# Two-layer conv, pooling and expert-retrieval encoder on one core: part of a norm's summing moved to VectorE, reciprocal roots spread without diagonal matrices, pooled products and four convolution taps moved to ScalarE

## The reference

```python
for l in range(DEPTH):                                   # DEPTH = 2
    mod = cond @ w_ada[l] + b_ada[l]                     # six vectors: shift, scale, gate, twice
    h = modulate(rmsnorm(x, norm1_g[l]), sh1, sc1)
    z = h @ w_in[l]                                      # 1024 -> 1536
    ya = conv_mixer(z[..., :512], z[..., 512:1024], ...) # u = a * sigmoid(b); 31 causal taps; LayerNorm; silu
    yb = pool_mixer(z[..., 1024:], ...)                  # y = (pooled @ w_grp + b_grp) * scale, 4 groups of 128
    x = x + g1 * (concat(ya, yb) @ w_out[l])             # 1024 -> 1024
    h = modulate(rmsnorm(x, norm2_g[l]), sh2, sc2)
    x = x + g2 * peer(h, peer_wq[l], ...)                # top-16 retrieval from 16384 experts
return rmsnorm(x, final_g)
```

## Time and profile before

| what | value |
|---|---|
| median of 3 runs | 3412.71 us (3411.85 to 3416.69) |
| the profiled execution, its own time | 3411.68 us |
| its span, first to last instruction | 3409.5 us |
| PE busy | 3326.1 us, 98% of the span |
| DVE, ACT, POOL busy | 2399.7, 1142.2, 746.4 us |
| mean granted clock of PE | 0.99 |
| PE idle, all waits of the list together | 75 us |

### The profile page before, as it was taken

One profiled execution on the slowest core, in us unless ns is written; L12 is line 12 of the kernel. 1 busy time (PEld: TensorE's weight loads), 2 busy tenths in 40 slices (PEclk: granted clock), 3 DMA queues, 4 the chain that ended last, 5 costly groups with the idle time before them and its releaser, 6 DMA issues.

```text
span 3409.5 us, 55288 instructions
## 1 busy us (share of the span) xinstructions
PE 3326.1 (98%) x16402; PEld 2815.3 (83%) x16402; DVE 2399.7 (70%) x6143; ACT 1142.2 (33%) x1606; POOL 746.4 (22%) x445
## 2 busy tenths in 40 slices
PE   6989999999999999999999999999999999999998
PEld 4568888888888999999975788888888889999997
DVE  7972999699994456666686259924999844666665
ACT  3233222334443333333342332223444433333332
POOL 0033454400000013333101334442000000233330
PEclk8999999999999999999999999999999999999999
DMA  6163766445556668888721224444555476788884
GB/s 245 51 220 108 251 229 218 153 180 203 184 222 225 203 230 283 282 286 279 231 97 38 75 90 148 146 147 140 186 204 222 176 245 202 255 286 281 282 285 142
DMA packets 316570, 675.88 MB, mean 198 GB/s; under 512 B 28864, under 2 KB 176704, under 8 KB 314304
## 3 DMA queue, kind: packets, MB, share of 16 engines
q1 hardware_dynamic: 253248, 478.81, 42.6%
q10 hardware_dynamic: 40704, 128.88, 9.6%
q0 software_dynamic: 22528, 67.19, 5.2%
HBM read 546.66 MB, written 127.93 MB: 198 GB/s over the span
## 4 chain that ended last, share of the span: by engine, by line
PE 83%; DVE 11%; issue 4%; DMA 1%; ACT 1%; DVEq 0%; SPq 0%; ACTq 0%
PE bank L481 27%; PE bank L605 24%; PE bank L485 13%; PE bank L609 12%; PE bank L588 3%; DVE scratch L1201 1%; DVE scratch L1086 1%; PE bank L405 1%; DVE h L1179 1%; DVE h L1182 1%; DMA scratch<-ada_t 1%; DVE h L1178 1%; DVE h L1181 1%; DVE z_pad L1228 1%; DVE z_pad L1230 1%
## 5 line engine op out<-in xcount | busy, mean ns | idle before, releaser
L481 PE MATMUL bank<-h_hi,w_hi 128*128 128x512 f32 x2528 | 1000.2, 396 | 5.1 <-ACT scratch L644 2.3
L481 PE MATMUL bank<-h_lo,w_hi 128*128 128x512 f32 x2528 | 985.5, 390 | 0.0
L644 ACT ACTIVATE w_hi<-ring 128x1024 fp32r<-128x1024 f32 x584 | 614.5, 1052 | 1106.1 <-PE bank L485 1060.1
L605 PE MATMUL bank<-v_hi,w_hi 128*128 128x448 f32 x2032 | 742.1, 365 | 0.0
L605 PE MATMUL bank<-v_lo,w_hi 128*128 128x448 f32 x2032 | 742.1, 365 | 0.0
L865 POOL TENSOR_TENSOR w_lo<-ring,w_hi 128x1024 fp32r<-128x1024 f32 x172 | 446.4, 2596 | 855.7 <-ACT w_hi L644 855.5
L485 PE MATMUL bank<-h_hi,w_lo 128*128 128x512 f32 x2528 | 624.3, 389 | 0.0
L481 PEld LDWEIGHTS bank<-h_hi,w_hi 128*128 128x128 f32 x2528 | 474.8, 188 | 105.9 <-issue 4.9
L481 PEld LDWEIGHTS bank<-h_lo,w_hi 128*128 128x128 f32 x2528 | 474.8, 188 | 98.3 <-issue 2.4
L485 PEld LDWEIGHTS bank<-h_hi,w_lo 128*128 128x128 f32 x2528 | 474.5, 188 | 98.5
L886 POOL DMA_INDIRECT keys<-ga_scratch,keys x128 | 122.3, 956 | 1623.1 <-DVE v_lo L1323 1623.1
(11 more groups left out here) (169 smaller groups left out, 2458.8 us busy)
## 6 DMA issues: line engine op xcount, KB each, us to landing
ring<-u_t SPq DMA_DIRECT2D x256, 512.0 KB, 3.5
ring<-v_t SPq DMA_DIRECT2D x256, 512.0 KB, 5.8
ga_scratch<-norm_tmp ACTq DMA_DIRECT2D x256, 256.0 KB, 2.0
g_scratch<-scratch ACTq DMA_DIRECT2D x14, 4096.0 KB, 13.7
scratch<-ga_scratch SPq DMA_DIRECT2D x256, 224.0 KB, 4.1
scratch<-g_scratch SPq DMA_DIRECT2D x128, 448.0 KB, 4.2
scratch<-ada_t SPq DMA_DIRECT2D x76, 512.0 KB, 5.7
ring<-wq_t SPq DMA_DIRECT2D x32, 512.0 KB, 3.3
```

What stands on the lines that cost most here:

```text
L481: pe.matmul(to, w_hi[:, b, k * P:(k + 1) * P], part_h[:, k, :], start=(k == 0 and part_h is h_hi), stop=False)
L605: pe.matmul(bank[:, k, 0:TD], w_hi[:, b, k * P:(k + 1) * P], part_w[:, b, 0:TD], start=(first and part_w is v_hi), stop=False)
L644: return act.activation(to, of, ACT.Copy)
```

## The change

Norm 2: PE no longer sums every square. DVE adds the squares of tiles 1 to 5 (`ADDED`) into that of tile 0 while `wout` runs, one before each of the tiles 3 to 7, and PE sums three at the end (blocks 0, 6 and 7). All norms: L974 goes; PE spreads the roots with four matmuls whose stationary operand is one column repeated 128 times and whose moving operand is the identity. Norm 2's order on DVE: the roots come first, then layer 0's last modulation, the biases and the gains. The bias adding becomes another form of instruction. Mixers: ACT makes taps 0 and 1 of conv blocks 1 and 2 (`begin_taps`, after `win` tiles 6 and 11), and takes the pooled products twice out of PSUM, to `mix` and to `h_hi`, with a bias made beforehand.

```diff
+    ADDED = 5
-    GATED_AT = {18: 1, 32: 2, 48: 3}
+    GATED_AT = {18: 1, 34: 2, 50: 3}
+    BEGUN = 2
@@ PE, spread_roots
-                pe.wait_ge(diag_ready, n_root + 1)
-                pe.matmul(bank[:, 1, :], ones[:, :], norm_tmp[:, 0, :], start=True, stop=True).then_inc(spread, 1)
+                pe.wait_ge(roots_made, n_root + 1)
+                for a in range(TT):
+                    root_a = norm_tmp[:, 1, 2 * TT + a:2 * TT + a + 1]
+                    mm = pe.matmul(bank[:, 1, a * P:(a + 1) * P], root_a.to_broadcast([P, P]), ident[:, :],
+                                   start=True, stop=True)
+                mm.then_inc(spread, 1)
@@ PE, wout
-                    if n == 2:
-                        sum_square(2 * l + 1, 0)
-                    sum_square(2 * l + 1, n - 1)
-                sum_square(2 * l + 1, KC - 1)
+                pe.wait_ge(square_added, ADDED * l + ADDED)
+                for n, k in enumerate([0] + list(range(ADDED + 1, KC))):
+                    pe.wait_ge(squared, KC * (2 * l + 1) + (k + 1))
+                    mm = sums(sq, n, k, KC - ADDED - 1)
+                mm.then_inc(summed, 1)
@@ ACT, win and mixers
+                BEGIN_AT = {6: 1, N_WIN - 1: 2}
+                def begin_taps(j):
+                    act.wait_ge(u_ready, CONV * l + (j + 1))
+                    at = COL_CONVW + j * TAPS
+                    act.activation(conv_y[:, j, :], u_pad[:, j, 0:T], ACT.Identity, scale=small[:, at:at + 1],
+                                   bias=small[:, COL_CONVB + j:COL_CONVB + j + 1])
+                    if j >= 2:
+                        act.wait_ge(conv_ready, (CONV - 1) * l + (j - 1))
+                    act.activation(conv_y[:, CONV - 1, :] if j == 1 else conv_odd, u_pad[:, j, 1:1 + T], ACT.Copy,
+                                   scale=small[:, at + 1:at + 2]).then_inc(taps_begun, 1)
...
+                    if n in BEGIN_AT:
+                        begin_taps(BEGIN_AT[n])
...
+                act.wait_ge(pool_bias_ready, l + 1)
                 for g in range(CONV):
-                    act.wait_ge(mix_b_ready, CONV * l + (g + 1))
-                    copy(h_hi[:, CONV + g, :], mix[:, CONV + g, :]).then_inc(hi_ready_h, 1)
+                    act.wait_ge(pool_product, CONV * l + (g + 1))
+                    for to in (mix, h_hi):
+                        ins = act.activation(to[:, CONV + g, :], bank[:, 4 + g, :], ACT.Identity, bias=pool_bias[:, g:g + 1],
+                                             scale=small[:, COL_POOLS + g:COL_POOLS + g + 1])
+                    ins.then_inc(hi_ready_h, 1)
@@ DVE, rstd
-                dve.tensor_tensor(diag, ident[:, :].unsqueeze(1).to_broadcast([P, TT, P]),
-                                  r.unsqueeze(2).to_broadcast([P, TT, P]), ALU.mult).then_inc(diag_ready, 1)
@@ DVE, wout and norm 2
+                    k = n - 2
+                    if 1 <= k <= ADDED:
+                        dve.wait_ge(squared, KC * (2 * l + 1) + (k + 1))
+                        if k >= 2:
+                            dve.wait_ge(square_added, ADDED * l + (k - 1))
+                        dve.tensor_tensor(sq[:, 0, :], sq[:, 0, :], sq[:, k, :], ALU.add).then_inc(square_added, 1)
                     wait_product(dve, l, 0, stages["wout"] + n)
...
                     with dve.If(l < 1):
                         modulate_later(KC + 2 * n)
-                        modulate_later(KC + 2 * n + 1)
+                        if n < N_WOUT - 1:
+                            modulate_later(KC + 2 * n + 1)
+                norm_roots(l, 2 * l + 1, ROOTS * l + 2)
+                settle(dve)
+                with dve.If(l < 1):
+                    modulate_later(3 * KC - 1)
                 wait_later(3 * KC)
                 add_bias(3 * KC, 2 * KC)
                 gains(1, 4 * KC, COL_NORM2)
-                norm_roots(l, 2 * l + 1, ROOTS * l + 2)
                 scale(ROOTS * l + 2, coef[:, 1, :], scaled)
```

More of the change, by code:

```diff
@@ L131, in hybrid_encoder @@
         fold = sb("fold", [P, OWN])
+        pool_bias = sb("pool_bias", [P, CONV])
         row_base = sb("row_base", [P, 1])
@@ L213, in hybrid_encoder @@
         squared, summed, var_ready, root_ready = sem("squared"), sem("summed"), sem("var_ready"), sem("root_ready")
-        diag_ready, spread, down_done = sem("diag_ready"), sem("spread"), sem("down_done")
+        roots_made, spread, down_done = sem("roots_made"), sem("spread"), sem("down_done")
         scaled, h_ready = sem("scaled"), sem("h_ready")
@@ L228, in hybrid_encoder @@
         taps_made, conv_last, conv_part, last_ready = sem("taps_made"), sem("conv_last"), sem("conv_part"), sem("last_ready")
-        mix_a_ready, mix_b_ready = sem("mix_a_ready"), sem("mix_b_ready")
+        mix_a_ready = sem("mix_a_ready")
         hi_ready_h, lo_ready_h = sem("hi_ready_h"), sem("lo_ready_h")
@@ L245, in hybrid_encoder @@
         own_weighed = sem("own_weighed")
+        square_added = sem("square_added")
+        taps_begun, pool_bias_ready = sem("taps_begun"), sem("pool_bias_ready")
         out_ready, out_stored = sem("out_ready"), sem("out_stored")
@@ L902, in _ @@
             POOL_STEPS = sum(w.bit_length() - 1 + 2 for w in WINDOWS)
-            STEPS = 3 * 5 + 4 + (CONV - 1) * TAPS - SHARED + 1 + POOL_STEPS + TT * (5 * (SEGS + HEADS) + 12) + 14
+            STEPS = 3 * 4 + 4 + (CONV - 1) * TAPS - SHARED + 1 - (CONV - 2) * BEGUN + POOL_STEPS + TT * (5 * (SEGS + HEADS) + 12) + 14
             for s in range(RING):
@@ L972, in rstd @@
                 link(dve.scalar_tensor_tensor(t, t, -0.5, v, ALU.mult, ALU.mult))
[L973 to L975 removed]
+                dve.scalar_tensor_tensor(r, t, 1.5, r, ALU.add, ALU.mult).then_inc(roots_made, 1)
             def roots(n_root):
@@ L1015, in add_bias @@
                 def add_bias(first, n):
-                    link(dve.tensor_tensor(mod[:, first:first + n], mod_sum[:, first:first + n],
-                                           small[:, COL_BADA + first:COL_BADA + first + n], ALU.add))
+                    link(dve.scalar_tensor_tensor(mod[:, first:first + n], mod_sum[:, first:first + n], 1.0,
+                                                  small[:, COL_BADA + first:COL_BADA + first + n], ALU.mult, ALU.add))
                 def gains(which, col, gain):
@@ L1048, in _ @@
                 dve.wait_ge(pads_zeroed, l + 1)
+                dve.tensor_tensor(pool_bias[:, :], small[:, COL_POOLB:COL_POOLB + CONV],
+                                  small[:, COL_POOLS:COL_POOLS + CONV], ALU.mult).then_inc(pool_bias_ready, 1)
                 lows, taps = [RING], [0]
@@ L1056, in gated @@
                        .then_inc(u_ready, 1)
-                def pool_mix():
-                    for g in range(CONV):
-                        dve.wait_ge(pool_product, CONV * l + (g + 1))
-                        dve.tensor_scalar(mix[:, CONV + g, :], bank[:, 4 + g, :], small[:, COL_POOLB + g:COL_POOLB + g + 1],
-                                          small[:, COL_POOLS + g:COL_POOLS + g + 1], ALU.add, ALU.mult).then_inc(mix_b_ready, 1)
                 def lo_mix(n, k):
@@ L1073, in conv @@
                     dve.wait_ge(u_ready, CONV * l + (j + 1))
-                    for k in range(n_taps):
+                    odd = conv_y[:, CONV - 1, :] if j == 1 else conv_odd
+                    if j >= 1:
+                        dve.wait_ge(taps_begun, (CONV - 2) * l + j)
+                        taps[0] += BEGUN
+                    for k in range(BEGUN if j >= 1 else 0, n_taps):
                         w = small[:, COL_CONVW + j * TAPS + k:COL_CONVW + j * TAPS + k + 1]
-                        acc = conv_y[:, j, :] if k % 2 == 0 else conv_odd
+                        acc = conv_y[:, j, :] if k % 2 == 0 else odd
                         src = u_pad[:, j, k:k + T]
-                        if k >= 2:
+                        if k >= (2 * BEGUN if j >= 1 else 2):
                             dve.wait_ge(dve_step, STEPS * l + (FIRST + steps[0] - 1))
@@ L1093, in conv @@
                     dve.wait_ge(dve_step, STEPS * l + (FIRST + steps[0]))
-                    both = dve.tensor_tensor(conv_y[:, j, :], conv_y[:, j, :], conv_odd, ALU.add)
+                    both = dve.tensor_tensor(conv_y[:, j, :], conv_y[:, j, :], odd, ALU.add)
                     if n_taps < TAPS:
                         link(both)
-                        pool_mix()
                         dve.wait_ge(conv_part, l + 1)
```

3 lines of the change are left out of this document (1 added, 2 removed).

## The result

The changed kernel took 3394.17 us (median of 5 executions, 3392.57 to 3394.58) against 3413.91 (5 executions, 3411.85 to 3416.69): a ratio of 0.9941, 95% interval 0.9927 to 0.9956. The prediction was 3393.4. The profiled execution took 3394.17, with a span of 3392.0 us where the span before was 3409.5, so 17.5 us went in the trace and 19.7 by the medians, where 19.3 were forecast.

A forecast was written before the change was run, and what follows sets the result against it. PE, busy 98% of the span, was taken as the bound; 6.4 + 1.8 + 5.3 + 1.8 + 3.05 + 0.95 = 19.3 us off 3411.68 gives 3392.4, median 3393.4. Range 3389 to 3398 us, chance 0.70.

The forecast's parts named there:

- Mixers, pauses 6.4: Mixers: PE's idle before the last conv sum, 4.38 us in layer 0 and 2.03 in layer 1, goes.
- Mixers' clock, 1.8: Mixers behind the last conv sum: PE stays at full clock without the pauses, gaining 1.8 us for both layers, bounds 0 and 2.4.
- without pauses PE has no reason to fall there: Mixers behind the last conv sum: PE's clock would not drop to the 1.2 GHz level; part of the 1.8 us clock term.
- Layer 1, wout, 5.3: Layer 1's wout: six sums of 0.89 us leave the places between products, gaining 5.3 us, bounds 4.5 and 5.4.
- Layer 0, wout and norm, 1.8: Layer 0's wout and norm 2: DVE's 5.93 us tile exceeds PE's 5.44, so only 1.8 us is gained, bounds 0 and 9.
- the sign that I named: Layer 0's wout: x(7) would come near 0.3 us later against its first tile than before.
- Roots without diagonals, 3.05: All norms: dropping L974 gains 0.73 us once and 0.58 in each of four norms, 3.05 in all; bounds -7 and 3.7.
- the slow column: Rival in the norms' spreads: the repeated column loads slowly and each spread grows; chance 0.04 for no change, 0.04 for slower.
- The spread's clock, 0.95: Norm 2 of layer 1: with idle shrunk to about 3.2 us, the spread gains 0.95 us; bounds 0 and 0.95.
- The sum: Whole kernel: all terms together save 19.3 us, giving 3392.4 us profiled and a median of 3393.4.
- DVE does not follow PE: Denies the rival that DVE follows PE in layer 0's wout, giving 7.2 us more, 3386.2 us; chance 0.10.
- ScalarE's part is in time: Denies the rival that ScalarE's mixer work comes late, losing 8.2 us, 3401.6 us; chance 0.12 with other such losses.

The follow-up runs named there:

- e6: The changed kernel with norm 2's three sums in the order tile 6, added tile, tile 7; 3390.07 us, ratio 0.9930.
- e4: The changed kernel with both last modulations, the biases and the gains ahead of the roots in norm 2 again; 3394.25 us, ratio 0.9941.
- e8: The changed kernel with e6's order of sums and ScalarE splitting the coming tile ahead of the square in every wout step; 3394.26 us, ratio 0.9943.
- e10: e6 with layer 0's modulations moved one step back, one behind x(6) and two behind x(7); 3390.56 us, ratio 0.9932.
- e11: e10 with ScalarE's last split of wout also put ahead of the square of tile 7; 3390.47 us, ratio 0.9928.
- e2: The kernel before with the squares' part alone: five squares added on VectorE, three sums at wout's end; 3406.99 us, ratio 0.9980.
- e5: The changed kernel with 7 of 15 modulations between layer 0's wout tiles cut from 1024 columns to 16; 3385.89 us, ratio 0.9920.
- e1: The kernel before with the mixers' part alone: ScalarE begins two blocks' taps and takes the pooled products; 3409.80 us, ratio 0.9985.
- e3: The kernel before with only the roots' spread made of eight passes from a repeated column, without diagonals; 3407.95 us, ratio 0.9982.

## Why the prediction was right, and where it was not

**Mixers, pauses 6.4.** Right. PE had no idle time ahead of the last conv sum, and VectorE ended its part at 145.52. The margin was as thin as forecast: in e6 PE waited 0.25 us there.

**Mixers' clock, 1.8.** The sums and half products run at the full clock as predicted, and the size was right: in e6, where the last conv sum stands in a row of its own, it takes 149.11 - 145.33 = 3.78 us to the sums of squares, where it took 5.28 and 4.11. But more than the gain is given back at L469 and L472, 1.56 and 1.51 us. The step that failed is "without pauses PE has no reason to fall there": taken word for word it held, but PE fell at the next place instead. With L472 at 2.0, layer 1's first stretch gained 3.1 to 3.9 (e4 to e8, e10, e11), with it at 3.1 it gained 2.5; 3.0 was the sum of my terms.

**Layer 1, wout, 5.3.** Right: 5.34 in e2, pitch 5.44.

**Layer 0, wout and norm, 1.8.** The mechanism was right: VectorE's tile above PE's, PE idle for more than 5 us at the end, and e5 shows that the modulations are what costs it. The sizes were not. The tile took 5.72, not 5.93, since the held adding takes 203.14 - 200.37 = 2.77 by pitch, where I had 0.70 + 2.27 = 2.97. I had let VectorE reach x(2) earlier by just what the mixers gain, 4.38 + 1.44 + 0.58 = 6.4; from the start of `win` it came 8.2 us earlier, 178.65 - 42.43 against 186.20 - 41.79. Some 2 of this are the biases, which POOL no longer held (0.17 us for 2.13), and they were free because the clock was low (e5); in e11, at the full clock, x(2) came 6.3 earlier, as I had it. From there to x(7) it took 28.0, not 27.4. So the sign that I named, x(7) 0.3 us later against its first product, did not come: 206.69 - 168.84 = 37.85 us against 213.29 - 173.51 = 39.78, 1.9 earlier. And the norm behind x(7) was too short in my sum: I let L998 end 4.9 us behind x(7), by POOL's tile; it ended 5.94 behind, by three sums at the low clock that had waited for the fifth adding. e6 takes that wait away and has 210.64 - 205.84 = 4.80. I had named the idle and not what it does to the sums behind it.

The parts are not additive in layer 0. Its first two stretches gain 4.27 in e1, 1.20 in e2, 1.59 in e3, 7.06 together, and 8.71 in the changed kernel; the order of norm 2 is 0.4 to 0.5 of the difference (e4). I argue, but no run isolates it, that the rest is e1's earlier VectorE, which is of use only when PE's tile is short, as e2 makes it; part of that lead is the low clock's, which e1 and the changed kernel have there and e2 and e3 do not.

**Roots without diagonals, 3.05.** Too low: e3 has 4.45, of which 0.69 in norm 2 of layer 0, which I had left out, and 0.70 a norm instead of 0.58. From the spread's start to its use it takes 156.84 - 155.65 = 1.19 us, before 163.09 - 161.92 = 1.17: 0.02 more for the short passes, not my 0.15. The Trainium skill, "TensorE: Matmul & The Clock Gate", section "Back-to-back issue gap", gives 81 ns for a matmul of 128 columns and 131 for one of 512; the estimate from them is 0.19, and the measurement decides for 0.02. The eight passes of a repeated column took 1.16 us, two long ones 1.12, so the slow column is out as a rival.

**The spread's clock, 0.95.** Failed in this kernel: idle 3.31, the low level. Behind the same 3.31 the spread took 1.16 in e5, e6 and e10. The step that failed is the reading of the level from the length of the idle.

**The sum.** By the same cuts I had 8.2, 9.8, 0.73 and 0.58, and 0 at the start; measured are 8.71, 8.44, 0.57, 0.42 and -0.64. The total was right within 1.8 us partly by luck. In layer 1 the clock took 1.51 us at L469 and L472 and kept back the spread's 0.95, and yet the layer is only 1.4 us short of my 9.8. In layer 0 the 1.56 us that PE lost at L469 and L472 do not show, since VectorE's early start, which itself hangs on the low clock there, made up for them. No rival came: DVE does not follow PE, ScalarE's part is in time (its last pooled product is taken at 143.1, and PE wants the first at 146.5), the column is not slow.

## What to carry to other kernels

When a stage is bound by two engines that start it at different times, shift the later engine by its own releases and not by the other engine's gain, and look at which of its instructions stand next to a GpSimd tile. Work that moves from PE to VectorE pays only where VectorE's tile stays below PE's: give the last sums of a chain an order in which the first of them waits for the least. And do not count on a clock term: remove the pause for its own sake, and keep 1 to 2 us per low stretch in the range. Before a low stretch is counted as a loss, ask who sets the pace there: in layer 0 it slowed PE and kept POOL's tile out of VectorE's way.
